# Residual stages of an eight-core decoder trunk: squares summed over the 8 tiles on GpSimd, two statistics matmuls per token group, the inverse root kept in PSUM

## The reference

```python
def rms_norm(x, g):
    xf = x.astype(jnp.float32)
    y = xf * lax.rsqrt(jnp.mean(xf * xf, axis=-1, keepdims=True) + EPS)
    return (y * g.astype(jnp.float32)).astype(x.dtype)
...
    for l in range(DEPTH):                      # DEPTH = 4, D_MODEL = 1024, SEQ = 2048
        h = rms_norm(x, norm1_g[l])
        ...                                     # three mixers, gates
        mixed = g_a * y_a + g_b * y_b + g_c * y_c
        x = x + (mixed @ w_o[l]).astype(x.dtype)
        h2 = rms_norm(x, norm2_g[l])
        u, v = jnp.split(h2 @ ffn_w13[l], 2, axis=-1)
        x = x + ((jax.nn.silu(u) * v) @ ffn_w2[l]).astype(x.dtype)
    return x
```

## Time and profile before

| | us |
|---|---|
| median of 3 runs | 5359.88 |
| lowest and highest | 5344.55, 6067.29 |
| profiled execution, its time | 5342.38 |
| its span on core 0, the slowest | 5340.7 |
| spans of the 8 cores | 5317.4 to 5340.7 |
| TensorE busy | 4977.3 (93%) |
| VectorE, ScalarE, GpSimd busy | 2505.6, 2159.5, 530.4 |

### The profile page before, as it was taken

How to read it: one execution, slowest core, us unless ns; L and a number is a source line. 1 busy time by engine, 2 the same in 40 slices (tenths; PEclk the granted TensorE clock), 3 DMA queues, 4 the chain that set the end, 5 groups by cost and what they waited for, 6 DMA issues and landing times.

```text
span 5340.7 us, 80489 instructions; the slowest of 8 cores (5317.4 to 5340.7 us)
## 1 busy us (share of the span) xinstructions
PE 4977.3 (93%) x30229; PEld 2386.1 (45%) x30832; DVE 2505.6 (47%) x5056; ACT 2159.5 (40%) x3748; POOL 530.4 (10%) x729
## 2 busy tenths in 40 slices
PE   4899998999888999999989999999998999999999
PEld 1445443444444544444444554444443455443444
DVE  4777264212578626512267752641127774353111
ACT  4379342111337924311143883431115297332110
POOL 1122000000213100000021310000002121000000
PEclk9999999999999999999999999999999999999999
DMA  5310326323430041621434004262242301316123
GB/s 125 60 19 14 86 46 143 59 36 96 91 66 13 8 108 31 159 48 33 117 65 77 8 19 98 42 157 38 36 134 46 65 8 40 85 33 167 36 54 101
DMA packets 135139, 355.82 MB, mean 67 GB/s; under 512 B 20720, under 2 KB 21360, under 8 KB 125552
## 3 DMA queue, kind: packets, MB, share of 16 engines
q0 software_dynamic: 28432, 160.30, 17.7%
q1 hardware_dynamic: 106336, 190.35, 12.8%
HBM read 405.08 MB, written 67.11 MB: 88 GB/s over the span
## 4 chain that ended last, share of the span: by engine, by line
PE 72%; ACT 11%; DVE 9%; DMA 4%; issue 3%; SPq 1%; POOL 0%; DVEq 0%; ACTq 0%
PE psb L300 71%; ACT ET L314 5%; DMA XW<-yT 1%; DVE T L319 1%; ACT LRq L314 1%; DVE H L336 1%; DMA XT<-xT 1%; DVE MMt L319 1%; ACT L314 1%; DVE OB L319 1%; ACT KCV L342 1%; SPq L349 1%; DVE ET L319 1%; PE psb L304 1%; ACT SQb L314 1%
## 5 line engine op out<-in xcount | busy, mean ns | idle before, releaser
L300 PE MATMUL psb<-H,w_f 128*128 128x512 bf16 x5516 | 1210.8, 379 | 6.1
L314 ACT ACTIVATE ET<-psb 128x512 bf16<-128x512 f32 (+1 forms) x1776 | 922.6, 630 | 113.2 <-PE psb L300 103.7
L300 PEld LDWEIGHTS psb<-H,w_f 128*128 128x128 bf16 x5632 | 551.1, 98 | 664.5
L319 DVE TENSOR_TENSOR HID<-SU,psb 128x512 bf16<-128x512 f32 x352 | 242.0, 687 | 947.5 <-PE psb L300 947.5
L300 PE MATMUL psb<-HID,w_f 128*128 128x512 bf16 x2763 | 613.0, 379 | 2.8
L314 ACT ACTIVATE SU<-psb 128x512 f32<-128x512 f32 x352 | 210.2, 597 | 976.7 <-PE psb L300 976.6
L300 PEld LDWEIGHTS psb<-VSW,ET 128*128 128x128 bf16 x6592 | 392.0, 97 | 355.5 <-issue 97.3
L300 PE MATMUL psb<-VSW,ET 128*128 128x65 bf16 x6592 | 466.8, 194 | 54.4 <-DVE SM L329 24.1
L314 ACT ACTIVATE SG<-psb 128x512 f32<-128x512 f32 x384 | 229.1, 597 | 613.7 <-PE psb L300 610.8
L300 PEld LDWEIGHTS psb<-HID,w_f 128*128 128x128 bf16 x2816 | 275.5, 98 | 332.1
L300 PE MATMUL psb<-H,w_wa 128*128 128x512 bf16 x1488 | 374.7, 388 | 1.9 <-issue 0.9
(11 more groups left out here) (144 smaller groups left out, 6041.7 us busy)
## 6 DMA issues: line engine op xcount, KB each, us to landing
w_f<-p_f POOLq DMA_DIRECT2D x44, 1024.0 KB, 10.2
U<-U SPq DMA_DIRECT2D x512, 65.8 KB, 2.0
yT<-XW SPq DMA_DIRECT2D x128, 256.0 KB, 6.9
XT<-yT SPq DMA_DIRECT2D x128, 256.0 KB, 4.8
yT<-XT SPq DMA_DIRECT2D x128, 256.0 KB, 3.9
XW<-yT SPq DMA_DIRECT2D x96, 256.0 KB, 6.6
w_f<-p_f POOLq DMA_DIRECT2D x32, 704.0 KB, 7.5
w_wa<-p_wa POOLq DMA_DIRECT2D x16, 768.0 KB, 11.6
```

The costliest lines, as they stand in the source:

```text
L300: return self.add("pe", lambda e: e.matmul(out.ap, lhsT.ap, rhs.ap, start=start, stop=stop, **kw), reads=[lhsT, rhs], writes=[out])
L314: return e.activation(out.ap, in_.ap, func, **kw)
L319: return self.add(eng, lambda e: e.tensor_tensor(out.ap, in0.ap, in1.ap, op), reads=[in0, in1], writes=[out])
```

## The change

In `residual`, the square of tile 0 of a token group goes straight into an f32 accumulator `ACC`; the squares of tiles 1 to 7 go into two f32 slots `SQF`, and GpSimd adds each to `ACC`. After tile 7 GpSimd rounds `ACC` to bf16 (`SQHI`) and subtracts to get the rest (`SQLO`, bf16). Two matmuls with the constant tile, one for each part, give the mean. Ln and Exp work in place in the PSUM bank, and the norm application reads the inverse root from there. `fin` (the two matmuls, Ln, Exp) is emitted 23 units after the last tile in wo and 30 in FFN-down; the norm applications follow in parts of 2 tiles (wo) or 4 (FFN-down), each 8 units after the part before. Wo has a slot for every one of its 32 tiles (24 in `XW`, 8 in `XT`) and 10 loads ahead. FFN-down polls once more in the middle of each group. `SQLO` shares memory with the first slot of `SQF`; `SQF` lies where `RS` did, `ACC` where `SQ` did.

```diff
@@ -658,8 +658,8 @@
         P.act(RS[:, r, :], RS[:, r, :], AF.Exp, scale=-0.5)
         return r
 
-    def norm_apply(l, gcol, c, tg, k, r, XX=XT):
-        P.stt(H[:, c, tg, :], XX[:, k, :], prm(l, gcol + c), RS[:, r, :], ALU.mult, ALU.mult)
+    def norm_apply(l, gcol, c, tg, x, rs):
+        P.stt(H[:, c, tg, :], x, prm(l, gcol + c), rs, ALU.mult, ALU.mult)
 
     def first_norm(tg, bank):
         ks = []
@@ -673,16 +673,22 @@
             P.mm(bank[:, :], cb(K_O1024), SQ[:, q, :], start=(c == 0), stop=(c == 7))
         r = norm_rs(bank)
         for c in range(8):
-            norm_apply(0, P_N1, c, tg, ks[c], r)
-
-    def residual(gcol, group, scale, psr, banks, apply_to, XX, nx, pf, wait_units, hooks=None):
+            norm_apply(0, P_N1, c, tg, XT[:, ks[c], :], RS[:, r, :])
+
+    SQF = sb_at("SQF", [128, 2, 512], F32, O_RS)
+    SQLO = sb_at("SQLO", [128, 512], BF16, O_RS)
+    ACC = sb_at("ACC", [128, 512], F32, O_SQ)
+    SQHI = sb_at("SQHI", [128, 512], BF16, O_R + 90112)
+
+    def residual(gcol, group, scale, psr, banks, apply_to, slot, nx, pf, fin_units, go_units, go_n, hooks=None):
         its = [(tg, j) for tg in range(4) for j in range(8)]
         cnt = {"loaded": 0, "free": nx}
 
         def xload(upto):
             while cnt["loaded"] < min(upto, cnt["free"], 32):
-                tg, j = its[cnt["loaded"]]
-                P.dma(XX[:, cnt["loaded"] % nx, :], Xsrc(j, tg))
+                n = cnt["loaded"]
+                tg, j = its[n]
+                P.dma(slot(n), Xsrc(j, tg))
                 cnt["loaded"] += 1
         xload(pf)
         for n, (tg, j) in enumerate(its):
@@ -693,35 +699,38 @@
             if hooks and n in hooks:
                 hooks[n]()
             assert cnt["loaded"] > n
-            k = n % nx
+            x = slot(n)
             if scale is None:
-                P.tt(XX[:, k, :], XX[:, k, :], ps[:, :], ALU.add)
+                P.tt(x, x, ps[:, :], ALU.add)
             else:
-                P.stt(XX[:, k, :], ps[:, :], scale, XX[:, k, :], ALU.mult, ALU.add)
-            P.dma(Xdst(j, tg), XX[:, k, :])
+                P.stt(x, ps[:, :], scale, x, ALU.mult, ALU.add)
+            P.dma(Xdst(j, tg), x)
             if gcol is None:
                 cnt["free"] += 1
                 continue
-            q = sqr.next()
-            P.act(SQ[:, q, :], XX[:, k, :], AF.Square)
-            bank = PSB[banks[tg % 2]]
-
-            def stat(q=q, j=j, bank=bank):
-                P.mm(bank[:, :], cb(K_O1024), SQ[:, q, :], start=(j == 0), stop=(j == 7))
-            if j < 7:
-                P.after(wait_units, stat)
+            if j == 0:
+                P.act(ACC[:, :], x, AF.Square)
             else:
-                def fin(stat=stat, bank=bank, tg=tg):
-                    stat()
-                    r = norm_rs(bank)
-
-                    def go(half):
-                        for c in range(4 * half, 4 * half + 4):
-                            norm_apply(apply_to, gcol, c, tg, (tg * 8 + c) % nx, r, XX)
-                        cnt["free"] += 4
-                    go(0)
-                    P.after(wait_units, lambda: go(1))
-                P.after(wait_units, fin)
+                P.act(SQF[:, j % 2, :], x, AF.Square)
+                P.tt(ACC[:, :], ACC[:, :], SQF[:, j % 2, :], ALU.add, eng="pool")
+            if j == 7:
+                P.copy(SQHI[:, :], ACC[:, :], eng="pool")
+                P.tt(SQLO[:, :], ACC[:, :], SQHI[:, :], ALU.subtract, eng="pool")
+                bank = PSB[banks[tg % 2]]
+
+                def go(c0, bank, tg):
+                    for c in range(c0, c0 + go_n):
+                        norm_apply(apply_to, gcol, c, tg, slot(tg * 8 + c), bank[:, :])
+                    cnt["free"] += go_n
+
+                def fin(bank=bank, tg=tg):
+                    P.mm(bank[:, :], cb(K_O1024), SQHI[:, :], start=True, stop=False)
+                    P.mm(bank[:, :], cb(K_O1024), SQLO[:, :], start=False, stop=True)
+                    P.act(bank[:, :], bank[:, :], AF.Ln, bias=EPS)
+                    P.act(bank[:, :], bank[:, :], AF.Exp, scale=-0.5)
+                    for i, c0 in enumerate(range(0, 8, go_n)):
+                        P.after(go_units * (i + 1), lambda c0=c0: go(c0, bank, tg))
+                P.after(fin_units, fin)
         xstate["in_y"] = True
 
     QT = sb_at("QT", [128, 4, 4, 512], BF16, O_R)
@@ -773,7 +782,7 @@
     SQL = sb_at("SQL", [128, 4, 512], BF16, O_R + 113472)
     CW = sb_at("CW", [128, 4, 4, 8, 32], BF16, O_WR)
     LRb = sb_at("LRb", [128, 2, 512], F32, O_RS)
-    XW = sb_at("XW", [128, 16, 512], F32, O_R)
+    XW = sb_at("XW", [128, 24, 512], F32, O_R)
     HID = sb_at("HID", [128, 4, 22, 512], BF16, O_R)
     sgr = Ring(4)
     mmr = Ring(3)
@@ -1276,7 +1285,9 @@
 
         def group(ps, tg, j):
             gmm(ps, (w0, w1)[j // 4], 8, 512, (j % 4) * 128, lambda kc, t: MIXED[:, kc, t, :], tg)
-        residual(P_N2, group, 0.5, PsRing([0, 1, 2, 3, 4, 5]), (6, 7), l, XW, 16, 6, 9)
+        def slot(n):
+            return XW[:, n, :] if n < 24 else XT[:, n - 24, :]
+        residual(P_N2, group, 0.5, PsRing([0, 1, 2, 3, 4, 5]), (6, 7), l, slot, 32, 10, 23, 8, 2)
         W.done(l, "wo", 0)
         W.done(l, "wo", 1)
 
@@ -1304,9 +1315,12 @@
                 cache[j] = W.get(l, "f2", j)
             for kc in range(22):
                 P.mm(ps[:, :], cache[j][:, kc * 128:(kc + 1) * 128], HID[:, tg, kc, :], start=(kc == 0), stop=(kc == 21))
+                if kc == 11:
+                    P.poll()
             if tg == 3:
                 W.done(l, "f2", j)
-        residual(None if last else P_N1, group, None, PsRing([0, 1, 2, 3, 4, 5]), (6, 7), l + 1, XT, NX, 4, 23, None if last else {17: load_cs, 25: lambda: load_ke(l + 1)})
+        residual(None if last else P_N1, group, None, PsRing([0, 1, 2, 3, 4, 5]), (6, 7), l + 1, lambda n: XT[:, n % NX, :], NX, 4, 30, 8, 4,
+                 None if last else {17: load_cs, 25: lambda: load_ke(l + 1)})
 
     W.pump()
     for l in range(L):
```

## The result

| | before | after |
|---|---|---|
| profiled execution, its time (us) | 5342.38 | 5286.79 |
| its span, slowest core | 5340.7 (core 0) | 5285.2 (core 2) |
| wo stages (us) | 79.04, 74.46, 71.63, 79.27 = 304.4 | 65.63, 62.68, 62.79, 68.72 = 259.8 |
| FFN-down stages with a norm | 159.26, 158.42, 158.42 = 476.1 | 153.24 x 3 = 459.7 |
| projection stages of layers 2 to 4 | 114.64, 113.79, 112.26 = 340.7 | 120.38, 115.93, 115.67 = 352.0 |

The ratio of after to before is 0.9878, 95% interval 0.9844 to 0.9912: 1.2% faster, and within 2%. A stage reaches from the first matmul of its kind to the first of the next.

The account below looks back on a forecast made before the run. TensorE, busy 93% of the span, was taken as the bound. From 5342.4 us, less 46 (wo) and 15.5 (FFN-down), plus 12 lost behind FFN-down, came 5293; the forecast was set at 5300, its own range 5275 to 5325.

Parts of the forecast that it names:

- wo, gain: Four output-projection stages: floor 226.3 plus 21 waits, 3 late loads and 8 slow clock, 258 us, gain 46 (30 to 78).
- FFN-down, gain: Three FFN-down stages with a norm: 24 fewer statistics matmuls each, 5.2 us per stage, 15.5 us in all.
- projection stages, loss: Behind FFN-down: TensorE's new wait for the VSW memset plus clock, 4 us per layer, 12 us lost (0 to 20).
- Prices: Instruction times assumed in wo: GpSimd addition 1.25 us, rounding copy 0.70, subtraction 1.20; VectorE application now 0.75, nothing to gain.
- The end of a token group: In wo, GpSimd's chain ends late: TensorE waits 0, 2.3, 2.6 and about 0.4 us, 5.3 per stage, 21 in all.
- VectorE's lateness itself stops nothing: In wo, TensorE has six banks, five groups or 8.6 us, so VectorE falling behind costs no wait.
- Late loads: First and last layer's wo: additions 1 to 2 us late behind FFN weights, 1.5 us per stage, 3 in all.
- Slow clock: Wo keeps eight waits of a length that costs 1.7 us in 5 of 10 cases; 8 us taken (0 to 14).
- GpSimd's queue at the layer's end: After FFN-down, the VSW memset stands behind the last tile's addition, copy and subtraction: 3.3 us new wait per layer.
- The chain is in time: Rival, chance 0.2: short GpSimd operations or VectorE catching up leave nearly no waits in wo; total 5255 us.
- The DMA is the bound: Rival, chance 0.12: at 220 GB/s the first and last layer's wo stages take 74.5 us, not 65; total 5319.
- GpSimd becomes the bound: Rival, chance 0.08: wo additions waiting behind VectorE cost 2.5 us each, a stage 88 us instead of 76; total 5387.

Follow-up runs that it names:

- e4b: Changed kernel with one norm application per group of matmuls in wo's first three token groups, at full clock; wo 238.4 us in sum on core 0.
- e3: Changed kernel with VSW's memset on VectorE and FFN-up's ring of banks starting at bank 2; shortest time on record 5277.0 us.
- e5: Changed kernel with 16 tiles loaded ahead in wo instead of 10; wo stages 62.69, 62.73, 62.67 and 62.84 us on core 0.
- e8: Changed kernel with one application per group, 16 tiles ahead, VSW's memset on VectorE, FFN-up's ring from bank 2; ratio to the kernel before 0.9808.
- e6: Changed kernel with wo's inverse root written to SBUF and read there by the norm applications; wo 275.9 us in sum on core 1.
- e9: Kernel before with 32 slots, 10 loads ahead and norm applications one per group (two in the last token group) in wo; time 5307.07 us.
- e2: Kernel before with only 32 slots and 10 loads ahead in wo; time 5351.1 us.

## Why the prediction was right, point by point

5300 was forecast (5293 on the scale of the profiled execution), 5286.8 came. The terms:

| term | predicted | measured |
|---|---|---|
| wo, gain | 46 (sum 258) | 44.6 (sum 259.8) |
| FFN-down, gain | 15.5 | 16.4 |
| projection stages, loss | 12 | 11.3 |
| all else | 0 | 5.8 gain |

By the averages of eight cores the gains are 47.4 and 15.7, the loss 10.0, and all else 0.4 the other way. So the 5.8 and 0.7 of the 16.4 are single cores' scatter.

- **Prices.** Addition 1.25, measured 1.27; copy 0.70, 0.61; subtraction 1.20, 1.155; application 0.75 or less, 0.744. The nearest rows of the trace were good to 15%.
- **The end of a token group.** Waits of 0, 2.3, 2.6 and 0.4 us were predicted for the four. In the second layer they were 0, 2.40, 1.39 and 0, in the third 0, 2.42, 0 and 0. The second is right in cause (e4b) and size. The third and fourth are over-sized: I took 2.16 us for VectorE's slot with two applications, and it is 2.04, half a microsecond less over four slots; what else shortens the third wasn't tried.
- **"VectorE's lateness itself stops nothing"** is the step that failed, by 6 us. I counted six banks. FFN-up starts its ring at bank 0 again, and wo's tile 30 had used that one: at the seam there is one group of slack and not five. It cost 1.5 us in each of the four layers, and it went when the ring started at bank 2 (e3) and as well when VectorE was on time (e4b): it takes both, the lateness and the short ring.
- **Late loads** in the outer layers were set at 1.5 us each; these stages are 3 and 6 us longer than the middle ones, and e5 takes exactly that away. That the sum came so near is luck in part, as over- and undersizing cancelled: waits for SQHI and SQLO, late loads with them, 21 + 3 = 24 us predicted and 14.2 + 4.7 = 18.9 measured; the bank 0 predicted and 6.1 measured; 24 against 25.0.
- **Slow clock.** 8 us predicted; the stages less the floor and less all waits leave 2.9 + 0.7 + 2.2 + 2.5 = 8.3. The 0.7 of the second isn't clock, which was 1.00 there.
- **GpSimd's queue at the layer's end.** 3.3 us per layer for the VSW memset predicted, 3.5 to 3.7 measured, and 4.1 had back when the memset moved (e3). Two things that the sum left out are in the second layer's 5.7: the late tile, 1.7, and more slow clock than the 0.7 assumed, as behind the 3.69 us 11 matmuls take 4.90 us, where 10 distances of 0.2159 and a last of 0.38 make 2.5.
- **Rivals.** "The chain is in time": wrong for the change as it is, but reached with one application per group, where wo is at the floor. "The DMA is the bound": wrong; the changed kernel's own first stage moves its 16.5 MB in 65.6 us at 252 GB/s, where I had carried over 220, and e8's runs at 262. The rate of a stage that waits is no ceiling. "GpSimd becomes the bound": its mechanism exists, as e6 shows, and the change avoids it. Let in, it cost 20 us in wo and 8 in FFN-up against the changed kernel, which leaves wo 27.5 us under the kernel before, and not 48 over it as that rival had it: most of the stretching falls on VectorE (96 applications, 0.30 us each) and little on GpSimd (112 additions, 0.10 each).

What the prediction didn't ask is what the gain needed. By e9 the old statistics with more slots and evenly spread applications save 51.8 us in wo; with e2, 12 to 13 of them are the slots' and 39 to 40 the spreading's. On the cores at full clock its whole span is as short as that of the change, with nothing on GpSimd and FFN-down untouched. The prediction let the old waits for squares go with the old matmuls; e9 keeps the matmuls, and the waits go all the same, since VectorE no longer does four applications in a row. The change has spread them only half way, two per group, and won 44.6. Its 96 fewer matmuls in wo (20.7 us) were paid back in waits; only with the applications spread fully do both add up, to 77.9 (e8, with the loads and the ring). The middle stages, where loads play no part, give the new statistics by themselves: 62.2 us with the old ones (e9), 56.7 with the new (e4b).

## What to carry to other kernels

Where an engine off the critical path gets extra work in bursts, compare its work per slot with the slot of the bounding engine (here 2.04 against 1.73 us): spreading eight instructions over eight slots instead of four removed every wait of the middle stages, without removing an instruction. When work moves to an idle engine, read what stands behind it in that engine's list, and at each seam between stages count the slack of a ring from the bank that was used last, not from the ring's size. Keep a second operand in PSUM when VectorE must run beside GpSimd. And compare a stage over all cores before a few microseconds of it are given to a cause: here one core's 15 us were 10.5 on average.

## What the runs showed of the hardware that I had not expected

- A norm application on VectorE with two SBUF tiles takes 1.045 us on average beside GpSimd's additions, and up to 1.76, and 0.744 without them (e6). GpSimd's 112 additions in wo take 1.367 us on average instead of 1.267, and the 84 in FFN-down stay at 1.264: most of the loss is VectorE's.
- The DMA engines moved 262 GB/s at a share of 1.00 in e8's first wo stage, against 220 at 0.92 in the same stage before. A share near 1 didn't mean that TensorE would wait.
- Short waits cost more than themselves. Before, the granted clock in wo was 0.91 to 0.98 with waits of about 2.2 us at each token group's end; with 0.6 to 2.5 us in which TensorE isn't busy in a whole stage (e9) and with none (e8) it was 1.00. What exactly makes it fall wasn't tried: of the 10 old waits of 2.2 to 2.8 us 5 were followed by a slow stretch, which cost 1.7 us, with nothing in the rows that tells them apart, and of the changed kernel's two middle stages, with the same 2.4 us of wait at the second token group's end, one kept 1.00 and the other fell to 0.97.
